# Joining the branches and projecting out with split operands in a trunk-layer kernel

## The reference, cut to what matters

```python
merged = sigmoid(ga) * (ya @ rwkv_w_proj) + sigmoid(gb) * (yb @ mlstm_w_proj)
x = x + gate1 * (merged @ w_out)
h = rmsnorm(x, norm2_g) * (1 + scale2) + shift2
x = x + gate2 * hier_moe(h)          # router logits = h @ [w_group | w_expert]
```

## Time and profile before

| what | us |
|---|---|
| median of 3 runs (2461.82 to 2471.61) | 2464.93 |
| the profiled execution, its own time | 2463.85 |
| its span, first to last instruction | 2462.3 |
| joining, between barriers | 160.0 |
| projection by tile, between barriers | 176.7 |
| TensorE busy in the span | 2069.9 (84%) |

### The profile page before, as it was taken

One profiled execution on the slowest core, in us unless ns is written; L12 is line 12 of the kernel. 1 busy time (PEld: TensorE's weight loads), 2 busy tenths in 40 slices (PEclk: granted clock), 3 DMA queues, 4 the chain that ended last, 5 costly groups with the idle time before them and its releaser, 6 DMA issues. The chain is left out here.

```text
span 2462.3 us, 56232 instructions
## 1 busy us (share of the span) xinstructions
PE 2069.9 (84%) x24073; PEld 1700.9 (69%) x24073; DVE 993.0 (40%) x2195; ACT 640.6 (26%) x1571; POOL 518.1 (21%) x638
## 2 busy tenths in 40 slices
PE   8899999888569963989989898899996399999940
PEld 8788888768446843989979797454454288788830
DVE  1566444246754425546546454421334000010036
ACT  2301112246445432334424232100111011111111
POOL 0000000008400027545746311111000300000012
PEclk9999999988878975999989899899997699999975
DMA  5233333214224242121111100333211499999944
GB/s 241 69 107 104 121 111 111 104 44 155 64 98 149 82 153 72 38 53 47 34 54 38 24 5 18 112 110 97 73 55 43 168 358 356 355 354 352 363 165 170
DMA packets 112789, 321.80 MB, mean 131 GB/s; under 512 B 19208, under 2 KB 65856, under 8 KB 101056
## 3 DMA queue, kind: packets, MB, share of 16 engines
q1 hardware_dynamic: 79392, 241.60, 27.7%
q0 software_dynamic: 11504, 42.00, 5.0%
q10 hardware_dynamic: 21680, 35.13, 4.2%
HBM read 252.26 MB, written 66.44 MB: 129 GB/s over the span
## 5 line engine op out<-in xcount | busy, mean ns | idle before, releaser
L2606 PEld LDWEIGHTS f_pab<-f_xt,f_w 128*128 128x128 f32 x2240 | 257.0, 193 | 17.4 <-issue 17.4
L2606 PE MATMUL f_pab<-f_xt,f_w 128*128 128x128 f32 x2240 | 257.3, 276 | 0.8 <-ACT f_xt L2636 0.8
L308 PE MATMUL b_ps<-b_h_hi,b_w_lo 128*128 128x512 f32 (+1 forms) x672 | 239.8, 357 | 8.3 <-DVE b_h_lo L382 8.3
L308 PE MATMUL b_ps<-b_h_lo,b_w_hi 128*128 128x512 f32 (+1 forms) x672 | 239.0, 356 | 0.0
L308 PE MATMUL b_ps<-b_h_hi,b_w_hi 128*128 128x512 f32 (+1 forms) x672 | 238.6, 355 | 0.0
L308 PEld LDWEIGHTS b_ps<-b_h_hi,b_w_lo 128*128 128x128 f32 x672 | 128.2, 191 | 26.1 <-issue 8.5
L308 PEld LDWEIGHTS b_ps<-b_h_hi,b_w_hi 128*128 128x128 f32 x672 | 128.1, 191 | 17.7
L308 PEld LDWEIGHTS b_ps<-b_h_lo,b_w_hi 128*128 128x128 f32 x672 | 128.2, 191 | 17.1
L2198 PE MATMUL e_pp<-y,e_wp 128*128 128x512 f32 (+1 forms) x384 | 137.7, 521 | 0.0
L1964 DVE TENSOR_TENSOR q_zz<-d_two_i,q_pn 128x128 f32<-128x128 f32 x400 | 100.1, 283 | 92.5 <-PE q_pn L1817 91.4
L2621 PE MATMUL f_po<-f_w,f_act 128*128 128x512 f32 x280 | 129.0, 603 | 3.8 <-issue 1.0
(11 more groups left out here) (458 smaller groups left out, 4365.0 us busy)
## 6 DMA issues: line engine op xcount, KB each, us to landing
f_w<-in_w SPq DMA_DIRECT2D x35, 2048.0 KB, 9.6
f_w<-in_w SPq DMA_DIRECT2D x35, 1024.0 KB, 9.8
ys_scratch<-f_out ACTq DMA_DIRECT2D x35, 512.0 KB, 9.0
b_wmod<-in_w_mod ACTq DMA_DIRECT2D x16, 1024.0 KB, 6.3
w_first<-in_w_in SPq DMA_DIRECT2D x14, 1024.0 KB, 4.8
sig_scratch<-b_stage POOLq DMA_DIRECT2D x20, 640.0 KB, 3.2
c_bc<-row_scratch SPq DMA_DIRECT2D x20, 512.0 KB, 3.7
su_scratch<-d_stage SPq DMA_DIRECT2D x16, 640.0 KB, 2.9
```

What stands on the lines that cost most here:

```text
L308: mm = pe.matmul(ps[j % 2][:, n, 0:width], rounded(wt[:, j // 2, k, (j % 2) * P:(j % 2 + 1) * P]), rounded(ht[:, k, first:first + width]), ...
L2606: mm = pe.matmul(pab[:, b, w, f * P:(f + 1) * P], w13[:, b, w, k, f * P:(f + 1) * P], xt[:, b, k], start=(k == 0), stop=(k == KD - 1))
```

## The change

Both phases take the three products of split operands. In the joining, `c.y` is split whole (three token blocks); the branch weights come in eight slices of 512 KB, one per output block, in a ring of three, and are split as they come. The modulation rows are no longer spread by TensorE: 64 columns are gathered, turned by one transpose, stored to memory, and read back by loads that repeat a row over the partitions; six such loads of 512 KB stand in the projection, two in the routing phase. The result is written over `c.y`.

In the projection `w_out` comes in 16 slices of 256 KB in a ring of two, each split by ScalarE and VectorE; each tile of `merged` is split two tiles ahead. `o_ht` has one buffer, residual input and normalised rows share one buffer of three, and L(t-2) stands ahead of P(t). The core of the diff:

```diff
 def phase_e_merge(c):
         def _(sp):
+            for f in range(3):
+                load_w(f)
             for n, (f, m) in enumerate(items):
...
+                if m == 0 and f >= 1 and f + 2 < KD:
+                    load_w(f + 2)
+                if n == 3:
+                    sp.wait_ge(rows_set, 1)
+                    sp.dma_start(c.mod_rows.rearrange("r (k n) -> (r k) n", n=P), turned_rows).then_inc(rows_stored, 16)
         def _(pe):
-            for n in range(len(reps)):
...
-                pe.matmul(pr[:, n % 2], c.ones[:, :], diag[:, n % 2], start=True, stop=True).then_inc(rep_ready, 1)
+            pe.wait_ge(gathered, 8)
+            pe.transpose(pr[0:64, 0:P], cols_of, c.ident[:, :]).then_inc(rows_turned, 1)
...
+                if f == 0:
+                    pe.wait_ge(y_split, m + 1)
+                pe.wait_ge(w_split, f + 1)
...
-                        mm = pe.matmul(pp[:, n % 2, x, 0:width], wp[:, x, k, f * P:(f + 1) * P], c.y[:, 4 * x + k, first:first + width],
+                        for i, (wt, yt) in enumerate(((w_lo, y_hi), (w_hi, y_lo), (w_hi, y_hi))):
+                            mm = pe.matmul(pp[:, n % 2, x, 0:width], rounded(wt[:, f % 2, x, k]), rounded(yt[:, 4 * x + k, first:first + width]),
         def _(dve):
+            w_rest(0)
+            y_rest(0)
...
+                    dve.tensor_copy(cols_of[:, 8 * (2 * r + s):8 * (2 * r + s) + 8], src).then_inc(gathered, 1)
+            y_rest(1)
+            y_rest(2)
+            w_rest(1)
...
+                if m == 2 and f + 2 < KD:
+                    w_rest(f + 2)
 def phase_e_rows(c):
         def _(sp):
+            for n, (half, k) in enumerate(slices):
+                if n >= 2:
+                    sp.wait_ge(wo_split, n - 1)
+                sp.dma_start(wo[:, n % 2], io["w_out"][:, k, 512 * half:512 * half + 512]).then_inc(wo_in[n % 2], 16)
+                if n == 1:
+                    for s in range(2):
+                        for r in range(3):
+                            sp.dma_start(rep[:, r, s], c.mod_rows[2 * r + s].partition_broadcast(P)).then_inc(rep_in, 16)
+                if n == 3:
+                    load_x(0)
...
         def _(pe):
             def project(t):
+                pe.wait_ge(m_split, t + 1)
...
+                        if t == 0:
+                            pe.wait_ge(wo_split, KD * half + k + 1)
+                        for i, (mt, wt) in enumerate(((m_lo, wo_hi), (m_hi, wo_lo), (m_hi, wo_hi))):
...
             for t in range(TILES + 2):
+                if t >= 2:
+                    logits(t - 2)
                 if t < TILES:
                     project(t)
                 if 1 <= t < TILES + 1:
                     turn(t - 1)
-                if t >= 2:
-                    logits(t - 2)
         def _(dve):
...
                     dve.tensor_tensor(x2[:, cols], x2[:, cols], xh[:, t % 3, cols], ALU.add).then_inc(x2_set, 1)
+                if t + 2 < TILES:
+                    m_rest(t + 2)
                 dve.wait_ge(squared, t + 1)
         def _(act):
...
+                act.activation(junk[:, :], c.x2[:, t], ACT.Square, accum_out=stat[:, 0, t:t + 1]).then_inc(squared, 1)
+                if t + 2 < TILES:
+                    m_high(t + 2)
                 act.wait_ge(var_set, t + 1)
                 act.activation(stat[:, 2, t:t + 1], stat[:, 1, t:t + 1], ACT.Sqrt).then_inc(std_set, 1)
                 if t >= 1:
                     turn(t - 1)
```

More of the change, by code:

```diff
@@ L2232, in _, with w_high, y_high, phase_e_rows @@
         def _(act):
[L2233 to L2239, removed]
+            def w_high(f):
+                act.wait_ge(w_in[f % 3], 16 * (f // 3 + 1))
+                if f >= 2:
+                    act.wait_ge(ready, 3 * (f - 2) + 3)
+                act.activation(rounded(w_hi[:, f % 2]), w[:, f % 3], ACT.Copy).then_inc(w_hi_set, 1)
+            def y_high(m):
+                first, width = BLOCKS[m]
+                act.activation(rounded(y_hi[:, :, first:first + width]), c.y[:, :, first:first + width], ACT.Copy).then_inc(y_hi_set, 1)
+            y_high(0)
+            w_high(0)
+            y_high(1)
+            y_high(2)
+            act.wait_ge(rows_turned, 1)
+            act.activation(turned_rows, pr[0:64, 0:P], ACT.Copy).then_inc(rows_set, 1)
+            for f in range(1, KD):
+                w_high(f)
+def phase_e_rows(c):
     nc, io = c.nc, c.io
@@ L2259, in phase_e_rows @@
+        wo_hi_set, wo_split, m_hi_set, m_split = (sem(n) for n in ("wo_hi_set", "wo_split", "m_hi_set", "m_split"))
+        projected, scaled, x2_set, squared, var_set, std_set, own_dve, h2_set = (sem(n) for n in (
+            "projected", "scaled", "x2_set", "squared", "var_set", "std_set", "own_dve", "h2_set"))
+        x_in, h2_stored = [sem(f"x_in{i}") for i in range(3)], [sem(f"h2_stored{i}") for i in range(3)]
         turned, ht_set, logit_ready, logit_set = (sem(n) for n in ("turned", "ht_set", "logit_ready", "logit_set"))
+        slices = [(half, k) for half in range(2) for k in range(KD)]
@@ L2285, in _ @@
+            for t in range(TILES):
+                store(t)
+                if 3 <= t + 2 < TILES:
+                    load_x(t + 2)
+            for i in range(3):
+                sp.wait_ge(h2_stored[i], 16 * ((TILES + 2 - i) // 3))
         @block.tensor
@@ L2291, in project @@
                         pe.wait_ge(scaled, n - 1)
-                    if n == 1:
-                        pe.wait_ge(w_in, 48)
                     for k in range(KD):
-                        mm = pe.matmul(po[:, n % 2], merged[:, k, t * P:(t + 1) * P], wo[half][:, k],
-                                       start=(k == 0), stop=(k == KD - 1))
+                        if t == 0:
+                            pe.wait_ge(wo_split, KD * half + k + 1)
+                        for i, (mt, wt) in enumerate(((m_lo, wo_hi), (m_hi, wo_lo), (m_hi, wo_hi))):
+                            mm = pe.matmul(po[:, n % 2], rounded(mt[:, t % 2, k]), rounded(wt[:, half, k]),
+                                           start=(k == 0 and i == 0), stop=(k == KD - 1 and i == 2))
                     mm.then_inc(projected, 1)
@@ L2311, in logits @@
                 pe.wait_ge(ht_set, 2 * t + 2)
+                if t == 0:
+                    pe.wait_ge(r_in, 32)
                 if t >= 2:
@@ L2327, in _, with wo_rest, m_rest, logit @@
             own = Own(dve, own_dve)
+            def wo_rest(n):
+                half, k = slices[n]
+                dve.wait_ge(wo_hi_set, n + 1)
+                dve.tensor_tensor(rounded(wo_lo[:, half, k]), wo[:, n % 2], wo_hi[:, half, k], ALU.subtract).then_inc(wo_split, 1)
+            def m_rest(t):
+                dve.wait_ge(m_hi_set, t + 1)
+                dve.tensor_tensor(rounded(m_lo[:, t % 2]), merged[:, :, t * P:(t + 1) * P], m_hi[:, t % 2], ALU.subtract).then_inc(m_split, 1)
+            def logit(t):
+                dve.wait_ge(logit_ready, t + 1)
+                dve.wait_ge(r_in, 32)
+                dve.tensor_tensor(c.logits[:, t], br, pl[:, t % 2, 0:20], ALU.add).then_inc(logit_set, 1)
+            m_rest(0)
+            for n in range(len(slices)):
+                wo_rest(n)
+                if n == KD:
+                    m_rest(1)
+            dve.wait_ge(rep_in, 96)
             for t in range(TILES):
@@ L2345, in _, with wo_high, m_high @@
                 own.settle()
+                own.did(dve.scalar_tensor_tensor(xh[:, t % 3], x2, stat[:, 3, t:t + 1], rep[:, 2, s], ALU.mult, ALU.mult))
+                own.settle()
+                dve.tensor_tensor(xh[:, t % 3], xh[:, t % 3], rep[:, 1, s], ALU.add).then_inc(h2_set, 1)
                 if t >= 2:
[L2347 to L2354, removed]
+                    logit(t - 2)
             for t in range(TILES - 2, TILES):
-                logit(dve, t)
+                logit(t)
         @block.scalar
         def _(act):
+            def wo_high(n):
+                half, k = slices[n]
+                act.wait_ge(wo_in[n % 2], 16 * (n // 2 + 1))
+                act.activation(rounded(wo_hi[:, half, k]), wo[:, n % 2], ACT.Copy).then_inc(wo_hi_set, 1)
+            def m_high(t):
+                if t >= 2:
+                    act.wait_ge(projected, 2 * (t - 2) + 2)
+                    act.wait_ge(m_split, t - 1)
+                act.activation(rounded(m_hi[:, t % 2]), merged[:, :, t * P:(t + 1) * P], ACT.Copy).then_inc(m_hi_set, 1)
             def turn(t):
@@ L2362, in turn @@
                     act.wait_ge(turned, 2 * t + half + 1)
-                    if t >= 2 and half == 0:
-                        act.wait_ge(logit_ready, t - 1)
-                    act.activation(ht[:, t % 2, 4 * half:4 * half + 4], pt[:, half], ACT.Copy).then_inc(ht_set, 1)
+                    if t >= 1 and half == 0:
+                        act.wait_ge(logit_ready, t)
+                    act.activation(ht[:, 4 * half:4 * half + 4], pt[:, half], ACT.Copy).then_inc(ht_set, 1)
+            m_high(0)
```

(8 more changed lines are left out.)

145 lines of the change are left out of this document (72 added, 73 removed).

## The result

| | before | after |
|---|---|---|
| median, runs on the same chip | 2468.27 us (4 runs) | 2510.74 us (4 runs, 2507.34 to 2516.12) |
| ratio, 95% interval | | 1.0185 [1.0167, 1.0202] |
| profiled execution | 2463.85 us | 2516.12 us |
| joining | 160.0 us | 124.9 us |
| projection | 176.7 us | 257.6 us |

The changed kernel is slower by 1.85%, 42 us. The two profiled executions lie 52.3 us apart: joining -35.1, projection +80.9, 4.6 in the stretch ahead of the joining, which no edit touches, and 1.9 behind routing.

What follows compares the result with a forecast made beforehand. TensorE was taken to set both stages, its queue showing one to one in the time. From 2463.85 us, joining 33 less and projection 79 more gave 2510 us, range 2488 to 2529.

Steps and rivals of the forecast that it cites:

- the side that had 0.93: Whole kernel: slower than before by more than about 0.5% (12.3 us), chance 0.93; the same 0.04, faster 0.03.
- Price of the products: Both stages: three products of 512 columns cost 0.68 us against 0.86 for one plain float32 product, a fifth less.
- Rival (c): Both stages: products cheaper than in the first projection, so faster than before; at 0.131 us each, 2417 us; chance 0.02.
- Joining: Joining stage: 126.7 us against 160.0, 33 us less, with 9.7 us instead of 18.5 ahead of the first product.
- Projection's start: Projection up to its first transposes T(0): 56 us instead of 31, 25 us lost, waiting for w_out slices behind loads.
- Rival (b): Projection's start slower: repeated rows loaded one after the other (+14 us) and slices at 3.8 us (+5); 2529 us; chance 0.09.
- Rounds: Projection, T(0) to T(8): TensorE stands 6.1 us per round and the clock falls; 23.35 us against 16.40, 184.5 us together.
- Rival (a): Projection's rounds: clock stays up through the stops, a round 19.6 us, eight of them 30 us less, 2480 us; chance 0.06.
- rival (d): Projection's rounds: m_high and m_rest beside the chain and the clock holding, a round 17.3 us, 2464 us, no change; chance 0.03.
- End and routing: Last transposes T(8) to routing 15.3 us against 16.1; routing's two gate2 loads hidden, 4 us if without cover.
- the bounds for the square into PSUM: Projection: writing the square's output to PSUM instead of SBUF, bounded by -0.1 and +0.3 us per tile, taken as nothing.

Runs made afterwards that it cites:

- experiment 1: The changed kernel with TensorE's old order: router matmuls L(t-2) again behind projection products P(t) and transposes T(t-1); 2437.05 us, 0.9885 of the kernel before.
- experiment 3: The changed kernel with 25 extra products of 448 columns behind each tile's transposes, into columns nobody reads, filling TensorE's stop; 2487.03 us.
- Experiment 2: The changed kernel with m_high moved behind ScalarE's copies and m_rest behind the normalised rows, off the path from transposes to router matmuls; 2488.72 us.
- experiment 4: The kernel before with only the router matmuls L(t-2) moved ahead of projection products P(t); plain products, no splits; 2529.41 us, one run.
- experiment 5: The changed kernel with the six repeating loads sent behind the last w_out slice instead of the second; 2520.39 us.

## Why the prediction was right

The forecast was 2510.0 us; the median is 2510.74, inside the range, on the side that had 0.93. Term by term:

- **Price of the products.** In the changed kernel 512 columns step by 0.227 us; I took 0.228. The Trainium skill's 131 ns sustained (TensorE: Matmul & The Clock Gate, Back-to-back issue gap) showed in no row here, though experiment 1 keeps TensorE busy without a gap for 106.8 us; its isolated figure, 216 ns, is the nearer. Rival (c) falls with it.
- **Joining.** 124.9 against 126.7 us. The start was the main term off: 8.55 us instead of 9.7, since the first slice landed sooner than the 4 us that I had put, 3.3 us into the stage (ScalarE copies it at 1561.24). For 1024 columns I had put 1.0 us a copy and 1.2 us a subtraction; the earlier trace rows give 0.89 and 1.10, and the single ones here took 1.06 and 1.22.
- **Projection's start.** T(0) 57.2 us in, against 56, but by two errors that nearly cancel. The six repeating loads held slice 2 to 16.1 us instead of 12.5, between the bounds of 10 and 23 us for them (my 9 us took the lower one, and the sum had no term for issuing them, 4.5 us), and P(0) ended at 46.3 us instead of 43. Then P(1) ran its 10.9 us at full clock, without the 2 us that I had added: though TensorE waited for 20.4 of the 42 us of P(0), the clock was full from 1726.7 on, in P(0)'s last products and all of P(1). Rival (b), 2529 us, falls; of the first of its two prices, 14 us, about a quarter came (3.6).
- **Rounds.** T(0) to T(8) 185.5 us against 184.5. The chain from T to L was 6.80 us against 7.05. The clock fell at every stop, as forecast, but not by the same amount: the seven full rounds went from 22.7 us to 23.9, mean 23.5, where I had 23.35 for each; the last took 20.7 against 21.05. The Trainium skill, same page, section HAM oscillation, describes a loop that stalls in each step, there for loads, and pays the low clock each time; the trace agrees, with 0.67 to 0.56 behind the stops for ScalarE's copies. Rival (a) had 19.6 us a round if the clock stayed up, and experiment 3 shows that round, 19.6 us, whenever the clock did stay up. So the price was right and the condition failed.
- **The shorter stop, rival (d).** It needed m_high and m_rest beside the chain and a clock that held. Experiment 2 built the first half; the clock fell all the same, and the round was 20.5, not 17.3 us.
- **End and routing.** 14.9 us against 15.3; routing 49.6 as before, so the two loads of gate2 are hidden as taken. No row of before gave the bounds for the square into PSUM, which I took as nothing; it took 1.03 us a tile instead of 1.06.

That the sum came within 1 us owes something to luck: the stretch ahead of the joining alone varies by 5, and from median to median the kernel lost 42.5 us where my terms add up to 46. The stages are the firmer evidence, but there too errors cancel: the joining came out 1.8 us shorter and the projection 1.6 longer than forecast, 382.5 us for the two together (124.9 + 257.6) against 382.7 (126.7 + 256).

The lower end of my range doesn't come out of its terms: -11 and -6 from 2510 give 2493, not 2488, and a clock back after 2 us would make a round 1.0 us shorter, not 1.35. The median is far from that end.

What is not settled: why the clock fell in every second round of experiment 3 from the third on, with products through nearly all of the stop. The engine did the transposes, wide products and the narrow L in each round alike. No run varied these one at a time.

## What to carry to other kernels

When an instruction is moved on an in-order engine, measure the chain that leads to it in the trace of before, even where that chain is fully covered: the 4.7 us from T to the end of the copies cost nothing there, and 57.6 us of the projection (experiment 4) once L stood ahead of the work that had covered them. Each stop of TensorE cost twice here, its own length and the products at half clock behind it, 6.0 and 3.9 us a round. And when a working set is cut into slices to make room, look for a buffer that is idle one stage earlier: together with loads sent in the order of need it gave back 31 us, where the one other order tried alone (experiment 5) lost 6.

## What was unexpected

- The rounds grew and then settled: 22.73, 23.29, 23.57 us, up to 23.87 and 23.83, with the granted clock behind L at 0.67 in the first and 0.56 in the fifth.
- Filling the stop did not hold the clock: with 6.2 of 6.8 us busy it still fell in every second round from the third on.
- In P(0) the granted clock changed back and forth while TensorE waited up to 2.5 us for a slice or pair: 1.00 from 1710 to 1715, 0.50 from 1716 to 1725.6, and 1.00 again from 1726.7; most of its products last 0.39 us each at the first level and 0.63 at the second.
- Six repeating loads of 512 KB sent at once landed 5.4 to 11.5 us after issue, and a 256 KB load sent behind them was ready for its copy 10.7 us after its issue (1688.24 to 1698.96), where such loads in twos otherwise land in 2.8 us.
